# All 31 taps of a depthwise convolution as matmuls with diagonals made by VectorE, in a two-block transformer kernel

## What is computed

```python
def conformer_conv(glu_in, dw, dw_b, ln_g, ln_b):
    a, gate = jnp.split(glu_in, 2, axis=-1)
    u = a * jax.nn.sigmoid(gate)
    u = lax.conv_general_dilated(
        u, dw[:, None, :].astype(u.dtype), window_strides=(1,),
        padding=[(CONV_WIDTH_2 - 1, 0)], dimension_numbers=('NWC', 'WIO', 'NWC'),
        feature_group_count=CONV_DIM) + dw_b.astype(u.dtype)
    return jax.nn.silu(layer_norm(u, ln_g, ln_b))
```

## Time and profile before

| | us |
|---|---|
| median of the runs | 1808.47 |
| the profiled execution | 1807.76 |
| its span, first to last instruction | 1806.0 |
| PE busy | 1740.0 (96%) |
| DVE busy | 1336.2 (74%) |
| ACT busy | 1161.0 (64%) |
| POOL busy | 63.8 (4%) |
| mean granted TensorE clock | 0.985 |

### The profile page before, as it was taken

The page is one execution under the profiler, slowest core; times in us unless marked ns, Lnnn a source line. Parts: engine busy times, 40 slices in busy tenths (PEclk is TensorE's granted clock), DMA queues, the critical chain, the costliest instruction groups (busy, mean ns, idle before and its releaser), DMA issues.

```text
span 1806.0 us, 23347 instructions
## 1 busy us (share of the span) xinstructions
PE 1740.0 (96%) x8588; PEld 1427.8 (79%) x8588; DVE 1336.2 (74%) x1191; ACT 1161.0 (64%) x1179; POOL 63.8 (4%) x64
## 2 busy tenths in 40 slices
PE   7899999989999989889999999999999999999998
PEld 6677888877788876668888888888888888888886
DVE  5664444676554458568888898898888898888988
ACT  5545543665544358647777777777777776776775
POOL 1010000130000000020000000000000000000000
PEclk9899999999999999979999999999999999999999
DMA  9545553545556454139999989999999999999995
GB/s 340 168 151 177 186 187 123 175 154 163 189 184 192 158 174 129 39 124 360 374 326 371 366 326 365 349 346 367 344 353 370 329 370 364 325 366 348 345 368 224
DMA packets 230600, 481.74 MB, mean 267 GB/s; under 512 B 12020, under 2 KB 55560, under 8 KB 230544
## 3 DMA queue, kind: packets, MB, share of 16 engines
q1 hardware_dynamic: 220224, 470.99, 73.3%
q10 hardware_dynamic: 10320, 9.99, 1.7%
HBM read 479.08 MB, written 2.65 MB: 267 GB/s over the span
## 4 chain that ended last, share of the span: by engine, by line
PE 68%; DVE 5%; ACT 4%; issue 2%; ACTq 0%; DMA 0%; DVEq 0%; POOL 0%
PE bank L631 21%; PE bank L634 20%; PE bank L632 20%; PE bank L1179 2%; ACT w_hi L1744 1%; PE bank L1211 1%; PE bank L1066 1%; DVE x L2286 1%; DVE w_lo L2306 1%; PE bank L625 1%; DVE w_lo L1801 1%; ACT w_hi L1281 1%; ACT L1744 0%; ACT e L1363 0%; ACT dwq L1656 0%
## 5 line engine op out<-in xcount | busy, mean ns | idle before, releaser
L2306 DVE TENSOR_TENSOR w_lo<-raw,w_hi 128x2048 fp32r<-128x2048 f32 x336 | 764.3, 2289 | 118.5 <-ACT w_hi L1744 115.7
L1744 ACT ACTIVATE w_hi<-raw 128x2048 fp32r<-128x2048 f32 x336 | 639.3, 1920 | 173.3 <-PE bank L634 173.2
L1801 DVE TENSOR_TENSOR w_lo<-raw,w_hi 128x2048 fp32r<-128x2048 f32 (+3 forms) x118 | 256.0, 2173 | 150.9 <-ACT w_hi L1281 150.5
L631 PE MATMUL bank<-w_hi,xg_hi 128*128 128x512 f32 x896 | 355.7, 397 | 5.9 <-DVE w_lo L2306 4.4
L634 PE MATMUL bank<-w_hi,xg_lo 128*128 128x512 f32 x896 | 350.5, 391 | 0.0
L632 PE MATMUL bank<-w_lo,xg_hi 128*128 128x512 f32 x896 | 349.9, 391 | 0.0
L631 PE MATMUL bank<-w_hi,a_hi 128*128 128x512 f32 (+3 forms) x672 | 263.1, 391 | 12.5 <-DVE a_lo L2165 4.4
L1281 ACT ACTIVATE w_hi<-raw 128x2048 fp32r<-128x2048 f32 (+3 forms) x118 | 213.1, 1811 | 91.9 <-PE bank L634 85.5
L634 PE MATMUL bank<-w_hi,a_lo 128*128 128x512 f32 (+3 forms) x672 | 256.1, 381 | 0.0
L632 PE MATMUL bank<-w_lo,a_hi 128*128 128x512 f32 (+3 forms) x672 | 256.0, 381 | 0.0
L631 PEld LDWEIGHTS bank<-w_hi,xg_hi 128*128 128x128 f32 x896 | 169.0, 189 | 42.4 <-DVE w_lo L2306 7.3
(11 more groups left out here) (229 smaller groups left out, 1695.3 us busy)
## 6 DMA issues: line engine op xcount, KB each, us to landing
raw<-in_moe_w_gate SPq DMA_DIRECT2D x114, 1024.0 KB, 7.0
raw<-in_moe_w_up SPq DMA_DIRECT2D x113, 1024.0 KB, 7.1
raw<-in_moe_w_down SPq DMA_DIRECT2D x112, 1024.0 KB, 6.5
raw<-in_w_mlp SPq DMA_DIRECT2D x32, 1024.0 KB, 5.2
raw<-in_ffn_w_gate SPq DMA_DIRECT2D x22, 512.0 KB, 3.8
raw<-in_ffn_w_up SPq DMA_DIRECT2D x22, 512.0 KB, 4.8
raw<-in_ffn_w_down SPq DMA_DIRECT2D x11, 1024.0 KB, 4.8
raw<-in_w_in SPq DMA_DIRECT2D x10, 1024.0 KB, 12.2
```

The costliest lines, as they stand in the source:

```text
L631: pe.matmul(o, hi, h, start=start, stop=False)
L1744: act.activation(w_hi[:, g % NSPLIT, :], raw_at(g, GRAN), ACT.Copy).then_inc(hi_made, 1)
L1801: dve.tensor_tensor(w_lo[:, g % NSPLIT, 0:n], raw_at(g, n), w_hi[:, g % NSPLIT, 0:n].bitcast(F32), ALU.subtract).then_inc(lo_made, 1)
L2306: dve.tensor_tensor(w_lo[:, g % NSPLIT, :], raw_at(g, GRAN), w_hi[:, g % NSPLIT, :].bitcast(F32), ALU.subtract).then_inc(lo_made, 1)
```

## The change

Five things are done:

1. All 31 taps are TensorE's. Tap n of a tile goes to the quarters of the even or of the odd taps as before, 31 of them, sixteen even and fifteen odd. VectorE no longer has taps of its own.
2. The diagonals are made by VectorE, in units of 12, 12 and 7 taps for each tile, each unit by one multiplication of the 64 x 64 identity, repeated, with the tap weights, each repeated over 64 columns. There are 18 units in four buffers, two in `kT` and two in `dwq`; a unit is made once the unit four before it has been used (`taps_through` counts its matmuls).
3. ScalarE copies the first bank of a tile with the bias to `dwy`, and VectorE adds the second bank to it. ScalarE asks for the root once, on a 128 x 1 tile, before the squares, and for SiLU once behind the root.
4. The seven parameter loads are issued by GpSimd, between `norm(NMEM1)` and `norm(NMIX1)`.
5. TensorE's order: `in2(2)` stands before the transposes of `mk2`, `taps(0)` before `glu_t(2)`, and one of the two pieces of `out2_part(1, 0, ...)` behind the variance. On ScalarE `hi_to(g + 4)` stands before the copy of `mk2`.

The diff, shortened:

```diff
 DW_K = 31
 CONV_TILES = 6
-PE_TAPS = 20
-TAP_PAIRS = PE_TAPS // 2
-DIAG_PAIRS = 12
+TAP_PAIRS = (DW_K + 1) // 2
+DIAG_UNITS = ((0, 12), (12, 24), (24, DW_K))
+DIAG_BUFS = 4
 TAP_BANK = (2, 4, 0, 2, 0, 4)
...
-        diag = dwq[:].rearrange("p k s -> p (k s)").rearrange("p (n c) -> p n c", c=HD)
+        diag = [half.rearrange("p k s -> p (k s)").rearrange("p (n c) -> p n c", c=HD)
+                for half in (kT[:, 0:3, :], kT[:, 3:6, :], dwq[:, 0:3, :], dwq[:, 3:6, :])]
...
+        warm = sb("warm", [P, 2], stack=layer)
...
-        diag_made, dw_acc = sem("diag_made"), sem("dw_acc")
+        diag_made, dw_half, dw_acc = sem("diag_made"), sem("dw_half"), sem("dw_acc")
...
+        def taps_through(unit, n):
+            k, u = divmod(unit, len(DIAG_UNITS))
+            return k * ((DW_K + (n < 2)) // 2) + (DIAG_UNITS[u][1] + (n < 2)) // 2
...
-            for n in (NFFN0, NMEM1, NMIX1):
+            for n in (NFFN0, NMEM1):
                 norm(n)
+            for dst, src in LOADS["l2"]:
+                pool.dma_start(dst, src).then_inc(l2_in, 16)
+            norm(NMIX1)
...
                 pe.wait_ge(glu_x_in[k // 2], 32)
                 ba, bb = bank[TAP_BANK[k]], bank[TAP_BANK[k] + 1]
...
+                for u, (first, last) in enumerate(DIAG_UNITS):
+                    unit = len(DIAG_UNITS) * k + u
+                    d = diag[unit % DIAG_BUFS]
+                    pe.wait_ge(diag_made, unit + 1)
+                    for tap in range(first, last):
+                        quarters = ((0, glu, 0, 0, ba), (1, glu, HD, HD, bb)) if tap % 2 == 0 else \
+                            ((2, glu_x, 0, HD, ba), (3, glu_x, HD, 0, bb))
+                        for n, g, r, c, b in quarters:
+                            pe.matmul(b[c:c + HD, 0:S], d[r:r + HD, tap - first, :], g[r:r + HD, k, tap:tap + S],
+                                      start=tap < 2, stop=tap >= DW_K - 2).then_inc(tap_used[n], 1)
...
             in2(0)
             in2(1)
+            in2(2)
             pe.wait_ge(qk_made, 5)
             cols_t(at["mk2"]["t"], kvm2, [0, P])
-            in2(2)
             glu_t(0)
             in2(3)
             in2(4, mq2_t)
...
             probs_t(MEM2 + 1)
             in2(7)
             values(MEM2 + 1)
-            glu_t(2)
             pe.wait_ge(s_exp, 4 * len(PAIRS))
             taps(0)
+            glu_t(2)
             pe.wait_ge(p_sb, 2 * len(PAIRS))
             taps(1)
             taps(2)
...
             out2_part(0, 0, (1,))
-            out2_part(1, 0, (0, 1))
+            out2_part(1, 0, (0,))
             for k in range(CONV_TILES):
                 pe.wait_ge(sqc_made, k + 1)
                 mm = pe.matmul(bank[7][:, 0:S], onesm[:], dwq[:, k, :], start=k == 0, stop=k == CONV_TILES - 1)
             mm.then_inc(var_psum, 1)
+            out2_part(1, 0, (1,))
             out2_part(0, 0, (2, 3))
             out2_part(1, 0, (2, 3))
             out2_part(0, 1, range(4))
...
-            for dst, src in LOADS["l2"]:
-                act.dma_start(dst, src).then_inc(l2_in, 16)
...
             act.wait_ge(kv_act, 2)
             act.wait_ge(kv_dve, 2)
             square_heads(kvm2, 0, MEM_HEADS, None)
...
             hi_to(g + 3)
             out_in2(0)
+            hi_to(g + 4)
             t_copy(at["mk2"]["t"], memk[:], GMK1)
-            hi_to(g + 4)
             act.wait_ge(l2_in, 16 * len(LOADS["l2"]))
             gates(0)
             hi_to(g + 5)
...
             probs_copy(MEM2 + 1)
             crossed(1)
             hi_to(g + 9)
-            diagonals(0, 6)
             out_in2(3)
             mixed_hi(MEM2 + 1)
             gates(2)
-            diagonals(6, 12)
             crossed(2)
-            diagonals(12, 20)
             hi_to(g + 10)
-            diagonals(20, CONV_TILES * TAP_PAIRS)
-            for n in range(4):
-                act.wait_ge(tap_used[n], CONV_TILES * TAP_PAIRS)
+            for k in range(CONV_TILES):
+                for n in range(4):
+                    act.wait_ge(tap_used[n], taps_through(3 * k + 2, n))
+                act.activation(dwy[:, k, :], bank[TAP_BANK[k]][:, 0:S], ACT.Identity, bias=dwb[:, k:k + 1]).then_inc(dw_half, 1)
+            act.activation(warm[:, 0:1], eps[:], ACT.Sqrt)
             for k in range(CONV_TILES):
                 act.wait_ge(cent_made, k + 1)
                 act.activation(dwq[:, k, :], dwy[:, k, :], ACT.Square).then_inc(sqc_made, 1)
             act.wait_ge(var_psum, 1)
             act.activation(stat[:, 0, :], bank[7][:, 0:S], ACT.Sqrt, bias=eps[:]).then_inc(sd_made, 1)
+            act.activation(warm[:, 1:2], eps[:], ACT.Silu)
             for k in range(CONV_TILES):
                 act.wait_ge(ln_made, k + 1)
                 act.activation(dwq[:, k, :], dwy[:, k, :], ACT.Silu, scale=lng[:, k:k + 1], bias=lnb[:, k:k + 1])\
...
+            def diagonals(first, last):
+                for unit in range(first, last):
+                    k, u = divmod(unit, len(DIAG_UNITS))
+                    t0, t1 = DIAG_UNITS[u]
+                    if unit >= DIAG_BUFS:
+                        for n in range(4):
+                            dve.wait_ge(tap_used[n], taps_through(unit - DIAG_BUFS, n))
+                    part, cols = (list(d) for d in ident2[:].ap)
+                    eyes = bass.AP(ident2[:].tensor, ident2[:].offset, [part, [0, t1 - t0], cols])
+                    dve.tensor_tensor(diag[unit % DIAG_BUFS][:, 0:t1 - t0, :], eyes, bcast(dw[:, k, t0:t1], HD), ALU.mult)\
+                        .then_inc(diag_made, 1)
+            def sum_taps(k):
+                dve.wait_ge(dw_half, k + 1)
+                dve.tensor_tensor(dwy[:, k, :], dwy[:, k, :], bank[TAP_BANK[k] + 1][:, 0:S], ALU.add).then_inc(dw_acc, 1)
...
             sum_heads(N2MK)
             chained(dve.memset(glu[:, :, 0:DW_K - 1], 0.0))
             chained(dve.memset(glu_x[:, :, 0:DW_K - 1], 0.0))
             chained(dve.memset(onesm[:], 1.0 / (CONV_TILES * P)))
+            for r in (0, HD):
+                ins = dve.tensor_copy(ident2[r:r + HD, :], ident[r:r + HD, r:r + HD])
+            chained(ins)
             lo_to(g + 3)
             scale_heads(N2MK, kvm2, 0)
             out_in2(0)
             lo_to(g + 4)
             dve.wait_ge(l2_in, 16 * len(LOADS["l2"]))
+            chained(dve.tensor_copy(dw[:, :, 1::2], dw_x[:, :, 1::2]))
             gated(0)
-            dve.wait_ge(t_dve, dve_steps(at["glu0"]["t"] + 1))
-            other_taps(0, 0, 2)
+            diagonals(0, 2)
             out_in2(1)
             sum_heads(N2MQ)
             lo_to(g + 5)
-            other_taps(0, 2, 5)
+            diagonals(2, 4)
             maxima(MEM2)
             lo_to(g + 6)
             probs(MEM2)
...
             probs(MEM2 + 1)
             gated(1)
             mixed_lo(MEM2)
-            other_taps(0, 5, N)
             lo_to(g + 8)
             out_in2(3)
             mixed_lo(MEM2 + 1)
+            lo_to(g + 9)
+            diagonals(4, 5)
             gated(2)
-            lo_to(g + 9)
-            dve.wait_ge(t_dve, dve_steps(at["glu2"]["t"] + 1))
-            other_taps(1, 0, 7)
-            add_taps(0)
-            add_taps(1)
-            other_taps(1, 7, N)
-            add_taps(2)
-            other_taps(2, 0, 6)
-            add_taps(3)
+            diagonals(5, 7)
+            sum_taps(0)
+            diagonals(7, 10)
+            sum_taps(1)
+            diagonals(10, 13)
+            sum_taps(2)
+            diagonals(13, 16)
+            sum_taps(3)
             lo_to(g + 10)
-            other_taps(2, 6, N)
-            add_taps(4)
-            add_taps(5)
+            diagonals(16, 18)
+            sum_taps(4)
+            sum_taps(5)
             dve.wait_ge(mu_psum, 1)
             for k in range(CONV_TILES):
                 dve.tensor_tensor(dwy[:, k, :], dwy[:, k, :], bank[6][:, 0:S], ALU.subtract).then_inc(cent_made, 1)
```

More of the change, by code:

```diff
@@ L1661, in _ @@
             square_heads(kvm2, 0, MEM_HEADS, None)
-            for r in (0, HD):
-                ins = act.activation(ident2[r:r + HD, :], ident[r:r + HD, r:r + HD], ACT.Copy)
-            chained(ins)
             hi_to(g + 3)
             out_in2(0)
+            hi_to(g + 4)
             t_copy(at["mk2"]["t"], memk[:], GMK1)
-            hi_to(g + 4)
             act.wait_ge(l2_in, 16 * len(LOADS["l2"]))
@@ L2138, in gated @@
                 ins.then_inc(t_dve, 1)
-            def other_taps(p, first, last):
-                for i in range(PE_TAPS + first, PE_TAPS + last):
-                    for k in (2 * p, 2 * p + 1):
-                        u, y = glu[:, k, i:i + S], dwy[:, k, :]
-                        if i == PE_TAPS:
-                            ins = dve.tensor_scalar(y, u, dw[:, k, i:i + 1], dwb[:, k:k + 1], ALU.mult, ALU.add)
-                        else:
-                            dve.wait_ge(dve_own, own[0] - 1)
-                            ins = dve.scalar_tensor_tensor(y, u, dw[:, k, i:i + 1], y, ALU.mult, ALU.add)
```

(11 more changed lines are left out.)

1 line of the change is left out of this document (removed).

## The result

The changed kernel takes 1813.99 us in the median of 20 runs (1810.29 to 1816.9). The kernel before takes 1808.51 us, also in 20 runs. The ratio is 1.0026, 95% interval 1.002 to 1.0033: slower, with the lower end of the interval at the 0.2% that can be told. The forecast was 1813.5 us. One execution of experiment six's kernel (3555.98 us) and one of experiment eight's second kernel (3524.94 us) took about twice as long as all others, and the medians given for these two leave them out.

A forecast was written before the change was run, and what follows sets the result against it. TensorE, busy 96% of the span, was taken as the bound. -5.5 - 1.15 + 14.1 - 1.4 - 1 = +5.1 us on the profiled 1807.76 gave 1812.8, or 1813.5 us for a median; 8-in-10 range 1808.5 to 1818.

The forecast's parts named there:

- The start, -5.5 us: Memory keys: loads off ScalarE and `in2(2)` filling TensorE cut the time to the query transposes; bounds -3.5 and -7.
- the new wait: Start: `glu_t(0)` needs the bank of ScalarE's keys copy, now behind `hi_to(g + 4)`; 0.5 us on TensorE.
- The estimate of 0 for GpSimd: Start: seven DMA issues fit into the 179 us between two GpSimd norms, so they cost 0.
- The wait ahead of the taps, -1.15: Ahead of the taps: `taps(0)` before `glu_t(2)` removes TensorE's 1.15 us wait for a copy; bounds 0 and -1.15.
- the taps, +14.1 us: Taps: six tiles of 16 steps at 0.44 us take 42.2 us instead of 28.1; bounds +12.3 and +16.8.
- rival D: Taps: faster, waits for single diagonals set the 0.44 us pace; 0.38 us a step gives 1807.8; chance 0.07.
- VectorE's diagonals, 0: Taps: units of 0.9 and 0.6 us on VectorE hide under TensorE's 2.6 or 1.5 us of taps.
- Rival E: Taps: slower, VectorE becomes the bound and TensorE waits some 1 us at six tiles; 1819.5 us; chance 0.08.
- The norm's order, -1.4 us: Norm: one output projection piece behind the variance brings the root 1.4 us earlier; bounds -0.5 and -1.4.
- The clock, -1 us: Norm: with 3.0 us idle left, the fall to 1.2 GHz may lessen; between 0 and -2.4.
- Rival B: No tellable change: clock stays at 2.4 GHz, 15.5 steps a tile, no new wait at start; 1809.8 us; chance 0.22.
- The table loads, 0: Norm: root and SiLU table loads already lie under other waits, so asking earlier gives 0; bounds 0 and -0.3.

The follow-up runs named there:

- experiment six: The changed kernel with each of VectorE's 18 units of diagonals made twice: 1816.53 us, 1.0037 of the kernel before.
- experiment eight's second kernel: Kernel before plus GpSimd's loads, earlier `in2(2)` and `hi_to(g + 4)`, output projection piece behind the variance, six unread matmuls at the norm; taps unchanged: 1800.18 us, 0.9948.
- experiment two: Changed kernel with the seven loads back on ScalarE: 1817.85 us; kernel before with only those loads moved to GpSimd: 1803.58 us.
- experiment three: The changed kernel with `in2(2)` behind the transposes of `mk2` again: 1813.23 us, 1.0029 of the kernel before.
- experiment five: The changed kernel with 30 taps on TensorE and the last tap of each tile on VectorE: 1810.68 us, 1.0009 of the kernel before.
- experiment seven: The changed kernel with `glu_t(2)` ahead of `taps(0)` again: 1814.82 us, 1.0031 of the kernel before.
- experiment one: The changed kernel without its two early table requests (root and SiLU): 1812.64 us, 1.0026 of the kernel before.
- experiment nine: Experiment eight's second kernel with `taps(0)` ahead of `glu_t(2)`, ScalarE's diagonals and VectorE's taps brought forward: 1803.53 us, 0.9969 of the kernel before.

## Why the prediction was right, point by point

- **The start, -5.5 us.** Measured -5.70 to the query transposes, -6.00 to the last `values`, so the term was half a microsecond short. The bulk is the loads (experiment two: 5.2 us alone). The forecast credited TensorE's order with part of it; experiment three gives that order nothing that the medians show. It priced the new wait at 0.5, which is 0.34. The estimate of 0 for GpSimd held: the issues take 4.0 us of the 179 between its two norms.
- **The wait ahead of the taps, -1.15, and the taps, +14.1 us.** Together 12.95, measured 12.70. The taps alone are 42.03 - 28.1 = +13.9. The count of 16 steps and not 15.5 was the term that mattered, and experiment five shows the whole step. The pace is 0.435 us at all tiles, so rival D falls: sixty waits or three, the pace is the same. The 1.15 us went, but the order deserves only about 0.5 of it (experiment seven).
- **VectorE's diagonals, 0.** The units take 0.95 and 0.61 us, for 0.9 and 0.6 expected, with TensorE without idle time. Rival E falls for the taps, by experiment six. The same experiment shows where E was nearly right: ahead of the maxima most of what is added to VectorE comes through, 2.8 of 3.5 us.
- **The norm's order, -1.4 us.** Measured -1.36.
- **The clock, -1 us.** This term was too large. In the profiled execution it gave nothing: 14.50 us against 14.19. Over all traces the stretch is 13.65 us in the mean of the nine with the shorter hole, and 14.19 and 13.49 in the two with the hole of 4.4 us (the kernel before, and experiment two's with the move alone). That is a few tenths, not one microsecond: the clock fell in eight of nine, where 1 of the 2.4 us of a full fall asks for one in little more than half. Rival B asked for no fall and 15.5 steps, and had both wrong.
- **The table loads, 0.** Right by experiment one. The Trainium skill ("ScalarE: Activation LUTs", "What ACT_TABLE_LOAD costs") puts a switch at 2.66 us, load and drain. The load is 1.28 us here too, and no row shows the drain; the price on this path is 0, since the load passes while the activation waits.

With -6.00, +12.70, -1.36 and +0.31 the sum is 5.65 us, against 5.1 in the forecast and 5.5 in the medians. The mechanism of each large term held. That the total came within 0.5 us of the median is in part luck: the start and the taps came out 0.5 and 0.25 us better than forecast, and the clock 1.3 us worse.

## What to carry to other kernels

A change of several parts is worth taking apart: by the ratios, the loads alone gave 5.2 us and all the small edits with the fill 9.4, and the part with the most code cost 12.8. Before work moves from a less busy engine to TensorE, count the steps that it adds, at the pace measured there. An odd tap out costs a whole step, as two taps do. Before work moves onto an engine with idle time, look at what stands behind it in that engine's queue: not only where its result is used, but also where it is made.

## What was not expected of the hardware

- Behind a hole of 3.05 us ahead of the normalized tiles the clock fell to 1.2 GHz in eight of nine traces with the same instructions there, and not in the ninth: 12.35 to 14.50 us for the stretch. Six matmuls that nobody reads, which cut the hole to 0.47 us, left no fall in the three profiled executions that have them (12.54, 12.74, and 12.52 in experiment nine).
- GpSimd's issue of a DMA took about 0.5 to 0.76 us of its program; with ScalarE as issuer, the seven held its next activation back by over 4 us.
- Not every table load passes ahead of the wait. In the changed kernel the one for the first exponential of the memory attention started only at 678.47 us, behind 4.31 us of waiting for VectorE, with its activation at 679.77. No run tries an early request there.
- A product with both operands repeated along a stride of zero, 128x768 in float32, took 0.95 us; by its length and the 1.22 us for 1024 it would be 0.92.
